# Chunk-recurrence levels cut in two around the quarters of a block compressor, in a hybrid decoder step

## The reference, cut to what matters

```python
b = jnp.cumsum(fi, axis=2)
o_inter = jnp.einsum('bhtd,bhde->bhte', qi * jnp.exp(b), S)
att = jnp.einsum('bhtd,bhsd,bhtsd->bhts', qi, ki, decay)      # decay = exp(b_t - b_s), causal
o = o_inter + jnp.einsum('bhts,bhse->bhte', att, vi)
S = jnp.exp(b_last) * S + jnp.einsum('bhsd,bhse->bhde', ki * jnp.exp(b_last - b), vi)
```

```python
flat = blocks.transpose(0, 1, 3, 4, 2, 5).reshape(B, n_cmp, 2, N_KV_B, CMP_BLOCK * HD_B)
hid = jax.nn.gelu(jnp.einsum('bnkgf,kfh->bnkgh', flat, w1))
return jnp.einsum('bnkgh,khd->bnkgd', hid, w2)
```

## Time and profile before

| what | value |
|---|---|
| runs | 3183.11, 3173.63, 3172.37 us; median 3173.63 |
| the profiled execution | 3191.88 us, of them 3190.1 in the span of the core |
| PE busy | 3009.3 us (94%) |
| DVE, ACT, POOL busy | 1025.6, 612.0, 1079.0 us |
| mean granted clock of PE | 0.962 of full speed |
| levels 2 to 6 with halves 0 to 4 on PE | from 404.8 to 510.9 us of the span |

### The profile page before, as it was taken

One profiled execution on the slowest core, in us unless ns is written; L12 is line 12 of the kernel. 1 busy time (PEld: TensorE's weight loads), 2 busy tenths in 40 slices (PEclk: granted clock), 3 DMA queues, 4 the chain that ended last, 5 costly groups with the idle time before them and its releaser, 6 DMA issues.

```text
span 3190.1 us, 45958 instructions
## 1 busy us (share of the span) xinstructions
PE 3009.3 (94%) x20048; PEld 2822.2 (88%) x20048; DVE 1025.6 (32%) x1107; ACT 612.0 (19%) x1012; POOL 1079.0 (34%) x596
## 2 busy tenths in 40 slices
PE   7999879999998769999999999999899999999996
PEld 5999868887887429899999999989898999999996
DVE  5000373334443120333222222335515222222223
ACT  3100013545554110211111000221102000011112
POOL 6432132400000362343333333433444333333331
PEclk9999988978999779999999999999999999999998
DMA  3211323310000442111111111131021111111111
GB/s 127 74 48 56 111 75 92 117 47 1 1 1 21 134 136 87 34 53 47 46 46 46 46 46 46 33 120 47 20 94 47 47 46 46 46 46 46 46 39 53
DMA packets 197865, 184.70 MB, mean 58 GB/s; under 512 B 7301, under 2 KB 181634, under 8 KB 196394
## 3 DMA queue, kind: packets, MB, share of 16 engines
q1 hardware_dynamic: 187498, 149.25, 15.0%
q0 software_dynamic: 10240, 33.56, 3.6%
HBM read 161.88 MB, written 25.09 MB: 59 GB/s over the span
## 4 chain that ended last, share of the span: by engine, by line
PE 78%; issue 8%; DVE 7%; POOL 4%; ACT 2%; DMA 1%; another core or an unknown queue 0%; SPq 0%; POOLq 0%; DVEq 0%; ACTq 0%
PE psum L259 47%; PE psum L390 6%; PE psum L283 5%; PE psum L1296 4%; PE psum L1651 3%; PE psum L1630 2%; POOL srows L950 1%; PE psum L271 1%; POOL whl L229 1%; DVE ntmp L358 1%; PE psum L1979 1%; PE psum L1596 1%; PE psum L1280 1%; PE psum L305 1%; PE psum L1597 1%
## 5 line engine op out<-in xcount | busy, mean ns | idle before, releaser
L259 PE MATMUL psum<-xhi,whl 128*128 128x344 f32 x4704 | 874.9, 321 | 4.5 <-issue 2.3
L229 POOL TENSOR_TENSOR whl<-wraw,zeroc 128x1024 fp32r<-128x1024 f32 x186 | 355.9, 1913 | 1266.1 <-PE psum L259 874.0
L259 PEld LDWEIGHTS psum<-xhi,whl 128*128 128x128 f32 x4704 | 765.9, 188 | 5.5 <-issue 4.5
L259 PE MATMUL psum<-xlo,whl 128*128 128x344 f32 x2352 | 500.2, 321 | 0.0
L232 POOL TENSOR_TENSOR whl<-wraw,whl 128x1024 fp32r<-128x1024 f32 x186 | 451.1, 2425 | 14.6
L259 PE MATMUL psum<-ahi,whl 128*128 128x344 f32 x2304 | 427.4, 319 | 0.0
L259 PEld LDWEIGHTS psum<-xlo,whl 128*128 128x128 f32 x2352 | 398.9, 189 | 0.0
L259 PEld LDWEIGHTS psum<-ahi,whl 128*128 128x128 f32 x2304 | 373.1, 188 | 3.0 <-DVE hT L450 2.5
L441 DVE CAST ahi<-frel 128x1032 fp32r<-128x1032 f32 x64 | 178.4, 2788 | 520.1 <-ACT frel L434 520.1
L450 DVE TENSOR_TENSOR hT<-hT,psum 128x1032 f32<-128x1032 f32 x128 | 157.4, 1230 | 489.1 <-PE psum L259 427.0
L432 ACT ACTIVATE frel<-psum 128x1032 f32<-128x1032 f32 x64 | 66.2, 1034 | 1206.3 <-PE psum L259 1188.5
(11 more groups left out here) (361 smaller groups left out, 3375.4 us busy)
## 6 DMA issues: line engine op xcount, KB each, us to landing
wraw<-in_w_ffn SPq DMA_DIRECT2D x128, 512.0 KB, 3.8
wraw<-in_w_in_ab SPq DMA_DIRECT2D x26, 512.0 KB, 3.7
h_spill<-hT SPq DMA_DIRECT2D x2, 4128.0 KB, 12.9
hT<-h_spill SPq DMA_DIRECT2D x8, 1032.0 KB, 8.1
wraw<-in_w_in_c SPq DMA_DIRECT2D x16, 512.0 KB, 4.0
xtok<-in_x_prompt SPq DMA_DIRECT2D x2, 2048.0 KB, 12.9
wrow<-in_state_win_kv SPq DMA_DIRECT2D x4, 1024.0 KB, 19.7
wraw<-in_w_out_ab SPq DMA_DIRECT2D x8, 512.0 KB, 4.3
```

The source lines that it names most:

```text
L229: pool.tensor_tensor(whl[:, s, 0, :], raw, zeroc[:, 0:1].to_broadcast([P, UNIT]), ALU.add).then_inc(w_hi, 1)
L259: last = pe.matmul(psum[:, 3 * bset + c, 0:TC], w, rhs[ah][:, k0 + k, c * TC:(c + 1) * TC], start=(k == 0 and n == 0), stop=(k == kn - 1 a ...
```

## The change

PE runs only steps 0 and 1 of levels 2 to 6 in front of the half; steps 2 and 3 come in the middle of it. In levels 2 to 5 they stand behind quarter 1 and its transposes, in level 6 behind quarter 0 of half 4. The spreads keep their places behind quarters 0 and 2. The sum of squares moves from behind quarter 1 to behind quarter 2. On DVE `sample_state` of the first sample of levels 3 to 5 moves from behind places 2 and 3 to in front of them. No instruction is added or taken away.

```diff
@@ dve_mid
                 place(l, 0)
                 place(l, 1)
                 update(l, 0)
+                if l in (3, 4, 5):
+                    sample_state(3 * (l - 3))
                 place(l, 2)
                 place(l, 3)
-                if l in (3, 4, 5):
-                    sample_state(3 * (l - 3))
                 update(l, 1)
@@ pe_mid
-            def level(l):
-                for j in range(4):
+            def level(l, steps_=range(4)):
+                for j in steps_:
...
             def sample_sums(q):
-                if q == 1:
+                if q == 0:
+                    level(6, range(2, 4))
+                if q == 2:
                     pe.wait_ge(g_ssq, 1)
...
-            level(2)
+            level(2, range(2))
             pe.wait_ge(m_pv, 4)
-            half(0)
+            half(0, lambda q: level(2, range(2, 4)) if q == 1 else None)
+
+            def inside_level(l, q):
+                b = 3 * (l - 3) + 1 + q // 2
+                if q == 1:
+                    level(l, range(2, 4))
+                elif q < 3 and b < NB:
+                    spread(b)
+
             for l in (3, 4, 5):
-                level(l)
-                b0 = 3 * (l - 3)
-                spread(b0)
-                half(l - 2, lambda q: spread(b0 + 1 + q // 2) if q % 2 == 0 and b0 + 1 + q // 2 < NB else None)
+                level(l, range(2))
+                spread(3 * (l - 3))
+                half(l - 2, lambda q: inside_level(l, q))
                 if l == 4:
                     outputs(0)
-            level(6)
+            level(6, range(2))
```

## The result

| | kernel before | changed kernel |
|---|---|---|
| median of the runs (5 each) | 3173.63 us | 3197.33 us |
| lowest to highest | 3167.82 to 3183.11 us | 3196.56 to 3206.86 us |
| ratio after/before, 95% interval | | 1.0061 [1.0034, 1.0088] |
| the profiled execution | 3191.88 us, span 3190.1 | 3200.13 us, span 3198.3 |

The changed kernel is slower, by 19 us after the ratio (11 to 28 by its interval), 23.7 between the medians. The forecast was +8.1. The median of 3197.33 lies above the upper end of the range, 3193; the ratio applied to the median of before, 3173.63 x 1.0061 = 3193.0, lies on it.

What follows compares the result with a forecast made beforehand. PE, busy 94% of the span, was taken to bound the kernel. Terms 0.7 + 3.1 + 0.9 + 3.4 = +8.1 us on the profiled 3191.88, carried to the median as 3181.7; range 3169 to 3193, counted as no change (0.82).

Steps and rivals of the forecast that it cites:

- Level 2, price 0: Starting half 0 after step 9 gains nothing, since step 12 hangs on DVE's held-up first update; 0 us.
- The faster rival: Level 2: DVE's first update starts before POOL's multiplications, saving 8.0 us; sum +0.1, or -4.3 (3169.3 us); chance 0.12.
- Level 3, +0.7: PE waits for sample state 0 behind update 0, then runs mostly at half clock; level 4 begins 0.7 us later.
- the walk: Level 3, timed operation by operation on PE and DVE: spread 1 at 433.4 after 5.3 us idle, level 4 at 449.6.
- Level 4, +3.1: New PE waits of 1.15 and 2.2 us for sample states before spreads, less the old 0.24: 3.1 us slower.
- Level 5, +0.9: A new PE wait of 2.7 us at spread 7, while the 1.83 at step 22 goes: 0.9 us slower.
- The clock, +3.4: Levels 4 and 5: waits of 2.2 and 2.7 us each cost half of a 3.40 us half-clock stretch, together 3.4 us.
- The bound in which the 1.15 does it too, 5.1: Upper bound for half-clock cost: level 4's wait of 1.15 us also brings a half-clock stretch, 5.1 us in all.
- Level 6 and half 4, price 0: Steps 26 and 27 move into half 4, taking 2.08 us either way, with their inputs long done; 0 us.
- the last one of the sum: Adding +8.1 to the profiled 3191.88 us and carrying its 18.3 us excess over the median unchanged, giving 3181.7.
- the rival that had 0.22: Level 3: place 15's lateness was an accident of the profiled run; without it the change costs +15.7 us, 3189.3; chance 0.22.

## Why the prediction had the mechanism right and the sum too low

- **Level 2, price 0:** held. Step 12 begins 17.13 us after the first transposes, 17.12 before, and the split alone costs nothing. The faster rival needed place 8 to come 2.2 us earlier. It came 1.1 earlier (L1017 starts 6.0 us behind the first transposes in place of 7.1), still behind POOL's first multiplication, and L1017 took 8.08 us in place of 7.00.
- **Level 3, +0.7:** +1.1 in the forecast's comparison. Spread 1 begins 11.4 us behind step 12, as in the walk (433.4 - 422.0). The idle in front of it is 2.87 and not 5, since spread 0, the quarter and the transposes ran at half clock behind the wait of 4.93 (2.07, 2.10, 1.06 us): less idle, same start. The wait at spread 2 was to be 3.2 and is 3.23. The walk's last piece, from 445.4 to 449.6, is 2.5 us of work at full clock and 1.7 that the text does not name; by its size it is half clock, and the piece measured 3.8.
- **Level 4, +3.1:** waits of 1.12 and 2.16 for 1.15 and 2.2; less 0.24, 3.0. The level is 22.4 us long and not about 20, because the half clock behind these waits, which the sum had in its clock term, falls into it.
- **Level 5, +0.9:** a wait of 2.54 for 2.7, and the 1.83 gone: 0.7.
- **The clock, +3.4:** 3.2 in the first profile, after the waits that were named, and shown as a cost of its own by filling them. The bound in which the 1.15 does it too, 5.1, was nearer in later profiles: the quarter behind that wait was slow in three of the four kernels that have the change's wait of 1.1 there (2.98, 3.13 and 3.48 us). The Trainium skill (TensorE: Matmul & The Clock Gate, section "HAM oscillation — how this bites in real kernels") would leave these waits without a fall of the clock; the trace disagrees again, with half-clock quarters behind 2.16 and 2.54 us and full-clock ones behind 0.44 and 0.81 (and, in the kernel of levels 3 to 5 alone, behind 2.41).
- **Level 6 and half 4, price 0:** -1.5 in the one comparison. Over the profiles this part takes 24.7 to 27.9 us where the level is split and 26.2 to 27.8 where it is not, so that -1.5 is within the scatter; and the kernel with the splits of levels 2 and 6 alone has 98.80 against 98.46 us for the stretch. Nothing worth a term.

**The step that failed is the last one of the sum:** "That execution was 18.3 us above the median of 3173.63; I carry the difference over as it is." The execution had place 15 late by 4.3 us and the half clock behind it, 7.6 us together. The rest of the 18.3 has no term; the profiled execution of the unmoved kernel stood 8.3 above its own median with no late place in it. In an execution without the late place level 3 takes 19.26 us instead of 26.86, and the changed order, which waits for update 0 and sample state 0 there whatever the place does, can't make use of it. The stretch is 7.3 us longer than the base with the late place and 14.9 longer than the base without. That is the rival that had 0.22, priced at +15.7. In my judgement it should have stood above the forecast, with what was known of the excess of that execution over the median. That the five runs which set the median of before had no late place is inferred, from their time (3173.63, beside 3177.9 on the chip where four profiles have none); none of those runs was profiled.

The rival's word "accident" was wrong as well. The late place recurs: in the first profile of the kernel before and to within 0.13 us in the unmoved kernel on the third chip (437.37 and 437.24), and others were in all kernels of the second chip. It is absent from the changed kernel's first profile and from all four profiles of the first chip of the experiments, where the kernel before takes 3177.9 us; on the two others it takes 3199.2 and 3188.6, and every profile there has a late place at least in level 2. It is a property of some chips or executions, and goes with POOL's indirect loads. Nor does a base with late places bring the cost down to the 7.3 of the first comparison: on the second chip the changed kernel has one of its own in level 5 and is 13 us slower.

**What stays open.** The first measurement says 19 us (11 to 28), the later ones 13 (9 to 19) for the same kernel and 11 (7 to 16) for levels 3 to 5 alone. All three intervals hold the 14.9 of the stretch; I have no term for the rest of the 19, if there is one. Part of it may lie in the sparse attention, 357.40 us with 79.9 of them at half clock in the changed kernel's profile, 346.60 with 53.5 before; but the unmoved kernel had 355.5 and the changed one 349 in its second profile, so no link with the change is shown. Why the loads delay the places on some chips only, and by which path, wasn't settled either.

## What to carry to other kernels

Where an edit moves work between a producer and its consumer, walk the orders of *both* engines: a short operation that another engine waits for belongs ahead of a long one that nobody awaits yet, and here the loss hung on 1.11 us standing behind 2.6 to 2.9. Before a sum is carried to the median, look at the base a second time (the same kernel with nothing moved is enough): a wait that a trace puts down to nobody may be missing in the runs that set the median, and then a change that waits in the same place costs its full price. This is the likeliest reading here and not a proven one. And a short wait on the matmul engine has two prices, its idle time and the half clock behind it; in levels 4 and 5 the second was nearly as large as the first (3.2 and 3.7 us).

## What the runs showed of the hardware

- **Handoffs come late while POOL issues indirect loads.** A place on DVE starts 2 to 8 us after PE's last product for it, "remote", between the eight loads' first issue and 2 us behind their last (427.19 to 437.54: late at 437.24; held back to 441.45 to 451.19: late at 444.93 and 452.85). In the same stretches PE's own products are often broken by pauses marked "issue", of up to 1.1 us each. Both show in all eight profiles of two chips and in none of the four of the other.
- **The sparse attention's length scatters** from 343.3 to 357.4 us over fourteen profiles of kernels that are the same in it, and goes with the time at half clock in it (39.3 and 79.9 us at those ends). This is as large as the effect under study, and it is why the spans of two executions say less than the stretch.
- **Half clock followed waits of 2.16 and 2.54 us in each profile that has them, and one of 1.1 in three profiles of four; it did not follow one of 2.41.** There is no sharp size in these rows.
- **DVE's update waits out POOL's whole series.** L1017 took 6.9 to 8.9 us in all fourteen profiles where it fell into POOL's eight multiplications (8.1 us), and 1.20 for the same shape later; it ended about 1 us behind the last of them.
